# Expert list sorted within each half of the tokens in a two-layer decoder kernel

## What is computed

```python
def hier_moe(h, w_group, b_group, w_expert, b_expert, w_gate, w_up, w_down):
    ...
    g_idx = jnp.argmax(g_logits, axis=-1)                  # 1 of 4 groups
    e_prob = jax.nn.softmax(e_logits[rows, g_idx], axis=-1)
    top_p, top_i = lax.top_k(e_prob, TOP_K)                # 2 of its 8 experts
    top_p = top_p / jnp.sum(top_p, axis=-1, keepdims=True)
    weights = g_w[:, None] * top_p
    expert_id = g_idx[:, None] * EXPERTS_PER_GROUP + top_i
    ...
        xb = t[tok]                                        # the tokens of expert e
        y = (jax.nn.silu(xb @ w_gate[e]) * (xb @ w_up[e])) @ w_down[e]
        return y * wt[:, None].astype(y.dtype)
    ...
    out = jax.ops.segment_sum(ys.reshape(P, D), tok_buf, num_segments=N)
```

## Time and profile before

| | |
|---|---|
| Median of 3 runs | 1249.63 us (1246.39 to 1251.85) |
| The profiled execution | 1250.87 us, span 1249.1 us from its first to its last instruction |
| Mean granted clock of PE | 0.970 of full speed |
| PE busy | 1176.5 us, 94% |
| DVE busy | 695.7 us, 56% |
| ACT busy | 326.3 us, 26% |
| Read from HBM | 240.19 MB |

### The profile page before, as it was taken

How to read it: one execution, slowest core, us unless ns; L and a number is a source line. 1 busy time by engine, 2 the same in 40 slices (tenths; PEclk the granted TensorE clock), 3 DMA queues, 4 the chain that set the end, 5 groups by cost and what they waited for, 6 DMA issues and landing times.

```text
span 1249.1 us, 17564 instructions
## 1 busy us (share of the span) xinstructions
PE 1176.5 (94%) x5132; PEld 657.6 (53%) x5132; DVE 695.7 (56%) x1627; ACT 326.3 (26%) x731; POOL 46.3 (4%) x89
## 2 busy tenths in 40 slices
PE   6999999999789999999979999999996999999997
PEld 3854555456584444444448545555565934444443
DVE  3344664557675555555542365644676745555555
ACT  4225231023412222222142153211143122222221
POOL 7000000000005000000000000000000000000000
PEclk9999998999889999999989999989997999999999
DMA  9030013420305999999740300244004069999992
GB/s 298 25 121 15 1 45 89 184 88 1 132 37 172 387 423 421 423 421 423 296 146 4 132 1 1 68 135 202 1 1 169 1 273 422 422 421 422 421 422 120
DMA packets 52965, 243.14 MB, mean 195 GB/s; under 512 B 8480, under 2 KB 19008, under 8 KB 27552
## 3 DMA queue, kind: packets, MB, share of 16 engines
q1 hardware_dynamic: 49760, 240.40, 48.5%
q0 software_dynamic: 2560, 1.89, 0.8%
q10 hardware_dynamic: 576, 0.02, 0.0%
HBM read 240.19 MB, written 2.10 MB: 194 GB/s over the span
## 4 chain that ended last, share of the span: by engine, by line
PE 86%; DVE 7%; issue 2%; DVEq 2%; ACT 1%; DMA 1%; ACTq 0%; POOLq 0%
PE ps L2560 18%; PE ps L2146 10%; PE ps L2582 9%; PE ps L2372 8%; PE ps L2138 6%; PE ps L2531 5%; PE ps L2532 5%; PE ps L2116 4%; PE ps L2167 4%; PE ps L2517 2%; PE ps L2239 2%; PE ps L2420 2%; PE ps L2208 2%; PE ps L2516 2%; PE ps L2216 1%
## 5 line engine op out<-in xcount | busy, mean ns | idle before, releaser
L2560 PE MATMUL ps<-wgu,xw 128*64 128x512 f32 x1024 | 225.5, 593 | 1.2 <-issue 0.6
L1978 DVE TENSOR_TENSOR X<-ps,X 128x512 f32<-128x512 f32 x256 | 156.6, 683 | 12.5 <-issue 10.0
L2146 PE MATMUL ps<-hT,ring 128*128 128x512 f32 x352 | 157.6, 603 | 0.0
L2560 PEld LDWEIGHTS ps<-wgu,xw 128*64 128x64 f32 x1024 | 74.6, 137 | 145.9 <-issue 145.7
L2582 PE MATMUL ps<-wdn,hhT 128*64 128x512 f32 x512 | 120.1, 612 | 3.3 <-ACTq L1211 3.3
L2372 PE MATMUL ps<-ring,yT 128*128 128x512 f32 x256 | 119.4, 616 | 0.4 <-DVE X L1376 0.4
L2531 PE MATMUL ps<-yhi,Wt 128*128 128x512 f32 x256 | 106.5, 416 | 3.7 <-DVEq L1262 3.7
L2146 PEld LDWEIGHTS ps<-hT,ring 128*128 128x128 f32 x352 | 67.2, 195 | 77.6 <-issue 77.6
L2532 PE MATMUL ps<-ylo,Wt 128*128 128x512 f32 x256 | 100.9, 394 | 0.0
L1985 DVE TENSOR_TENSOR hh<-ps,silu 128x256 f32<-128x256 f32 x32 | 13.6, 425 | 126.9 <-ACTq L1205 126.9
L1996 DVE SCALAR_TENSOR_TENSOR ylo<-ps,ws,yhi 128x512 fp32r<-128x512 f32 x64 | 48.1, 751 | 63.9 <-ACTq L1221 63.9
(11 more groups left out here) (367 smaller groups left out, 1496.7 us busy)
## 6 DMA issues: line engine op xcount, KB each, us to landing
wgu<-in_w_gate SPq DMA_DIRECT2D x64, 1024.0 KB, 12.2
wgu<-in_w_up SPq DMA_DIRECT2D x64, 1024.0 KB, 14.4
wdn<-in_w_down SPq DMA_DIRECT2D x64, 1024.0 KB, 14.2
ring<-in_w_in SPq DMA_DIRECT2D x8, 1024.0 KB, 6.6
ring<-in_w_mix_out SPq DMA_DIRECT2D x12, 512.0 KB, 6.0
w_kv<-in_xa_w_kv SPq DMA_DIRECT2D x4, 1024.0 KB, 9.4
ring<-in_w_in SPq DMA_DIRECT2D x2, 2048.0 KB, 15.5
ring<-in_w_in SPq DMA_DIRECT2D x2, 1536.0 KB, 15.7
```

Source lines behind the costliest of these rows:

```text
L1978: tt(xh, bank, xh, ALU.add).then_inc(mfreed((what, n)), 1)
L2146: last = mm(bank, w[:, c, c0:c0 + P], hT[:, c, :], start=c == 0, stop=c == KD - 1)
L2560: last = mm(bank[r], xw[:, c, r], wgu[2 * parity + j][:, :, c, :], start=c == 0, stop=c == KD - 1)
```

## The change

The list is no longer sorted over all tokens. It is sorted within each half of the tokens: first all assignments of tiles 0 and 1, by expert, then those of tiles 2 and 3. So each half of the list has only its own two tiles as sources, and the gather makes 2 tiles x 8 groups x 2 parts = 32 products for each half. An expert's tokens then lie in two spans. `list_spans` writes for each expert the start of the first, the start of the second, and the count of the first (at most 64); ACT copies 64 columns from the first start, and then, over what lies behind the first span, 64 columns from the second start to the place given by the count (`from_first`, `from_second`). Beside this, DVE's order is another (the last two tiles' one-hots, `placed`, `overflow_tiles`, which computes two more columns), PE runs `slots()` behind step 0, `diag` and `ranked` lie elsewhere, and SP loads pair 1's weights at once. The diff, cut to its core:

```diff
-        xw = at("xw", [P, KD, P], F32, late + 4096)
...
+        xw = at("xw", [P, KD, 2, 2 * SLOTS], F32, late + 4096)
...
-        G = at("G", [P, 2, SEQ], F32R, late)
+        G = at("G", [P, 3, SEQ], F32R, late)
...
-                load_gate_up(l, 1, 1)
-                load_down(l, 1, 1, (0,))
-                multiplied(l, 0, ("wslot",))
-                load_down(l, 1, 1, (1,))
+                load_pair(l, 1, 1)
...
+                def from_first(j, e):
+                    s0 = act.value_load(spans[0:1, bass.ds(e, 1)], min_val=0, max_val=2 * SEQ)
+                    copy(xw[:, :, j, 0:SLOTS], xgT[:, :, bass.ds(s0, SLOTS)])
+
+                def from_second(j, e):
+                    s1 = act.value_load(spans[0:1, bass.ds(e + NE, 1)], min_val=0, max_val=2 * SEQ)
+                    n0 = act.value_load(spans[0:1, bass.ds(e + 2 * NE, 1)], min_val=0, max_val=SLOTS)
+                    copy(xw[:, :, j, bass.ds(n0, SLOTS)], xgT[:, :, bass.ds(s1, SLOTS)])
+
+                def windows_second(p):
+                    act.drain()
+                    for j in range(2):
+                        from_second(j, 2 * p + j)
+                    act.drain()
+                    act.nop().then_inc(S["xw_ready"], 1)
...
+                        wait_apart(act, S["G_used"], done(l, "G_used", 2))
+                        for j in range(2):
+                            from_first(j, j)
...
-                        windows(p + 1)
+                        for j in range(2):
+                            from_first(j, 2 * p + 2 + j)
...
                     act.nop().then_inc(S["hhT_ready"], 1)
+                    if ahead:
+                        windows_second(p + 1)
                     if isinstance(p, int) and p == 0:
+                        for k in range(2):
+                            bank = mfull(act, l, 0, ("places", k))
+                            copy(places[:, k], bank).then_inc(mfreed(("places", k)), 1)
+                            act.drain()
+                            act.nop().then_inc(S["places_ready"], 1)
...
-                copy(xw[:, :, SLOTS:2 * SLOTS], xgT[:, :, bass.ds(second, SLOTS)])
...
+                windows_second(0)
                 step_(0, 0, True)
...
+                nc.vector.tensor_tensor_scan(rt[:, 4, 1:n_lists], counted[:, 0:n_lists - 1],
+                                             rt[:, 2, NT:NT + n_lists - 1], 0.0, ALU.add, ALU.add)
                 dve.drain()
-                tt(r32(5), ranked_from, row(4).unsqueeze(1).to_broadcast([P, NT, NE]), ALU.add)
+                lists = rt[:, 4, 0:n_lists].rearrange("p (g e) -> p g e", g=HALVES)
+                tt(rt[:, 5].rearrange(by_half, g=HALVES, e=NE), ranked_from,
+                   lists.unsqueeze(2).to_broadcast([P, HALVES, NT // HALVES, NE]), ALU.add)
...
-                def one_hot(half, t):
-
-                    g = NT * half + t
-                    place = (dest, dest_2)[half]
-                    if g >= 2:
-                        dve.wait_ge(S["G_used"], done(l, "G_used", g - 1))
-                    ts(Gx[:], iota[:], place[:, 0, t:t + 1], None, ALU.is_equal)
-                    dve.drain()
-                    stt(G[:, g % 2], iota[:], place[:, 1, t:t + 1], Gx[:], ALU.is_equal, ALU.add)
+                def one_hot(t):
+
+                    place = (dest, dest_2)[t // (NT // HALVES)]
+                    hot = G[:, t % 3]
+                    if t >= 3:
+                        dve.wait_ge(S["G_used"], done(l, "G_used", t - 2))
+                    ts(hot, iota[:], place[:, 0, t:t + 1], None, ALU.is_equal)
+                    dve.drain()
+                    stt(hot, iota[:], place[:, 1, t:t + 1], hot.bitcast(F32), ALU.is_equal, ALU.add)
                     signal("G_ready")
...
+                def list_spans():
+
+                    dve.wait_ge(S["rank_kept"], done(l, "rank_kept", 1))
+                    ts(rt[:, 4, n_lists:n_lists + NE], first_count, float(SLOTS), None, ALU.min)
+                    tt(counts, first_count, rt[:, 1, NE:2 * NE], ALU.add)
+                    tt(rank[:, 2:4], rank[:, 2:4], first_count.unsqueeze(1).to_broadcast([P, 2, NE]), ALU.add)
+                    dve.drain()
+                    nc.vector.tensor_copy(spans, rt[:, 4, 0:3 * NE])
+                    signal("spans_ready")
...
+                    ts(expert, expert, float(NE - 1), None, ALU.min)
+                    for dst, of in ((first, first_from), (second, second_from), (split, split_from)):
+                        tt(passed, begun[:], of.unsqueeze(1).to_broadcast([P, OVF, NE]), ALU.mult)
+                        dve.drain()
+                        nc.vector.tensor_reduce(dst.unsqueeze(2), passed, AX_X, ALU.add)
...
                     if back:
                         bring_back(p, "comb", range(8))
                     else:
+                        placed()
+                        overflow_tiles()
                         slot_weights()
                         spread(parity)
                     for h in range(2):
...
-                one_hot(0, 0)
+                one_hot(0)
                 low_part(0)
-                one_hot(0, 1)
+                one_hot(1)
                 low_part(1)
                 ts(dest_2[:], dest[:], -float(SEQ), None, ALU.add)
-                nc.vector.tensor_copy(starts[:], row(4))
-                signal("starts_ready")
+                list_spans()
+                one_hot(2)
                 low_part(2)
-                one_hot(0, 2)
+                nc.vector.memset(xgT[:, :, 2 * SEQ:SORTED], 0.0)
+                sorted_gain(0)
                 low_part(3)
-                one_hot(0, 3)
+                one_hot(3)
+                sorted_gain(1)
+                tiles_past()
+                padded_places()
                 token_weights()
-                one_hot(1, 0)
-                sorted_gain(0)
-                one_hot(1, 1)
-                tiles_past()
-                one_hot(1, 2)
-                padded_places()
-                one_hot(1, 3)
-                nc.vector.memset(xgT[:, :, 2 * SEQ:SORTED], 0.0)
-                placed()
-                sorted_gain(1)
-                overflow_tiles()
                 step_(0, 0, False)
...
                 pe.wait_ge(S["rank_kept"], done(l, "rank_kept", 1))
-                for half in range(HALVES):
-                    for t in range(NT):
-                        if half == 0:
-                            wait_apart(pe, S["xhi_ready"], done(l, "xhi_ready", t + 1))
-                            if t > 0:
-                                wait_apart(pe, S["xlo_ready"], done(l, "xlo_ready", t + 1))
-                        pe.wait_ge(S["G_ready"], done(l, "G_ready", NT * half + t + 1))
-                        hot = G[:, t % 2]
-                        if t == 0:
-                            for c in range(KD):
-                                mm(mbank_of(l, 0, ("sorted", half, c)), xhi[:, t, c::KD], hot,
-                                   start=True, stop=False)
-                            if half == 0:
-                                wait_apart(pe, S["xlo_ready"], done(l, "xlo_ready", 1))
+                for t in range(NT):
+                    half, inner = t // per, t % per
+                    wait_apart(pe, S["xhi_ready"], done(l, "xhi_ready", t + 1))
+                    pe.wait_ge(S["G_ready"], done(l, "G_ready", t + 1))
+                    hot = G[:, t % 3]
+                    if inner == 0:
                         for c in range(KD):
-                            bank = ps[:, head.job["sorted", half, c][0], :]
-                            if t > 0:
-                                mm(bank, xhi[:, t, c::KD], hot, start=False, stop=False)
-                            last = mm(bank, xlo[:, t, c::KD], hot, start=False, stop=t == NT - 1)
-                            if t == NT - 1:
-                                last.then_inc(mfilled(("sorted", half, c)), 1)
-                        if t < NT - 1:
-                            last.then_inc(S["G_used"], 1)
-                        else:
-                            pe.drain()
-                            pe.nop().then_inc(S["G_used"], 1)
+                            mm(mbank_of(l, 0, ("sorted", half, c)), xhi[:, t, c::KD], hot, start=True, stop=False)
+                    wait_apart(pe, S["xlo_ready"], done(l, "xlo_ready", t + 1))
+                    for c in range(KD):
+                        bank = ps[:, head.job["sorted", half, c][0], :]
+                        if inner > 0:
+                            mm(bank, xhi[:, t, c::KD], hot, start=False, stop=False)
+                        last = mm(bank, xlo[:, t, c::KD], hot, start=False, stop=inner == per - 1)
+                        if inner == per - 1:
+                            last.then_inc(mfilled(("sorted", half, c)), 1)
+                    if inner < per - 1:
...
+                step_(0, 0, False)
                 slots()
-                step_(0, 0, False)
```

113 lines of the change are left out of this document (56 added, 57 removed).

## The result

The changed kernel takes 1234.54 us (median of 5 runs, 1226.14 to 1235.26) against 1249.63 (1246.39 to 1252.03) for the kernel before on the same chip: ratio 0.9863, interval 0.9838 to 0.9888. That is faster by 1.4%, inside the range that I gave and 2.8 us above the time that I named. Run a second time, beside the first three experiments, it gave 1233.85 (6 runs) and a ratio of 0.9856 [0.9829, 0.9883].

What follows compares the result with a forecast made beforehand. PE was taken to bound the kernel (86% of the last chain), the gather being its own. Twice -8.3 a layer plus 1.3 from transfers makes 17.9 us off 1250.87: 1233.0, named 1231.7 as median; range 1225 to 1239, chance 0.85.

Steps and rivals of the forecast that it cites:

- The sum per layer: Start of pair 1 in each layer: -14.7 + 4.7 + 1.7 = -8.3 us.
- Products removed and the gather's end: Gather on PE: 64 of 128 products go, 15.7 us; with stalls and drains the gather ends 14.7 us earlier per layer.
- The wait for ACT: Ahead of pair 0's gate/up: PE idles 4.9 us for ACT's copies and register loads, 4.7 more than before.
- The clock in that gap: PE's new empty gap ends at the low clock, costing 1.7 us on pair 0's gate/up, 8.7 instead of 7.05.
- The gap behind gate/up stays and pays its 1.69 as before: Pair 0's down products stay at the slow clock, 5.27 us against 3.58 in the loop.
- Step 0 on DVE: Overflow part grows to 9 us; `ylo` of pair 0 ready after 16.6, wanted after 19.1: covered, 2.4 to spare.
- signs of being wrong: Wrong if PE waits on `xw_ready` in the loop, or on `ylo_ready` in step 1.
- DVE's tail in step 0 is longer than its cover: Rival: overflow part 12 us, pair 1 waits 0.6, clock falls again, 2.3 a layer: 1236.3; chance 0.12 (shared with longer stalls).
- The loop: ACT's two more copies a pair cost nothing, with 0.7 us to spare before PE needs `xw_ready`; step stays 14.58.
- The transfers: Pair 2's load gains 3.7 us of lead, recovering the late last pairs' loss at the loop's end: 1.3 us in all.
- The 0.6 for `wgu`: Pair 15 of layer 0 waits 0.6 us for `wgu`, read as the transfers being late at the loop's end.
- DVE holds the gather's end: Rival: gather ends where it did, PE's saving turns into waits, 11.5 us slower, 1261; chance 0.02.

Runs made afterwards that it cites:

- first three experiments: placed_early, act_regs and pe_fill, edits of the changed kernel timed beside its second run; medians 1231.44, 1227.35 and 1231.08 us.
- act_regs: Changed kernel with pair 0's four second-window register loads moved on ACT to behind the wait for the spans; 1227.35 us, ratio to before 0.9802.
- pe_fill: Changed kernel plus 16 unread products on PE between the last gather product and the wait for xw_ready; 1231.08 us, ratio to before 0.985.
- slots_first: Changed kernel with slots() ahead of step 0 on PE again and placed() ahead of it on DVE; 1250.81 us, ratio to before 0.9999.
- combo: Changed kernel with placed_early, act_regs and no_drain joined, and xgT's tail memset moved behind one_hot(3) on DVE; 1223.15 us, ratio to before 0.9775.
- placed_early: Changed kernel with placed() moved on DVE to ahead of step 0; 1231.44 us, ratio to before 0.9852.
- fill_both: Changed kernel with pe_fill's 16 products and nine more unread products behind pair 0's gate/up; 1231.52 us, ratio to before 0.9834.
- no_drain: Changed kernel without PE's drain and signal ahead of the last pair's step, SP waiting for the same event instead; 1232.12 us, ratio to before 0.9857.
- more_copies: Changed kernel with ACT copying the second windows of pairs 1 to 15 twice, behind a drain; 1253.37 us, ratio to before 1.0015.
- late_load: Changed kernel with SP issuing pair 2's loads only when PE has done slots(); 1245.62 us, ratio to before 0.9961.

## Why the prediction was right, and which of its terms were not

The sum per layer was -8.3 us; to the start of pair 2 it was measured at -8.8 (67.62 to 58.83) and -8.7 (67.51 to 58.78). With the late steps that is 18.0 us, where the sum had 17.9; the medians are 15.1 and 17.0 apart, and what lies outside the two stretches varies by 7.8 us between two executions of the changed kernel (726.1 and 733.9). Point by point:

*Products removed and the gather's end*: -14.7 predicted, -14.5 measured (33.72 to 19.25). The stalls are where I put them: tile 2's eight products took 3.36 instead of 1.96, and PE waited 0.40 for the last one-hot.

*The wait for ACT*: 4.9 predicted, 4.40 measured, gate/up 23.65 us after the first gather product where I had 23.9. act_regs shows that the register loads are part of it.

*The clock in that gap*: gate/up 8.7 predicted, 8.76 to 8.79 measured, and once 9.25; pe_fill shows that the idle gap is the cause.

*"The gap behind gate/up stays and pays its 1.69 as before"*: **this step failed.** Down took 3.65 and not 5.27. The runs show one fall for the two gaps: where the first was filled, the second paid (pe_fill, 5.35 twice; before, 5.27 and 5.24), where the first paid, the second did so in two of twelve, and where both were filled none did. (slots_first, with its other order, has a long gate/up and a long down in layer 0, 9.54 and 4.98; in layer 1 `slots()` alone is long, 5.8.) In act_regs neither paid, with gaps of 2.60 and 2.96 us (the two small products within it counted), and combo's gap of the same 2.60 fell in one layer of two. So the length of a gap in these rows doesn't decide it alone. The Trainium skill's page "TensorE: Matmul & The Clock Gate", section on the HAM clock gate, has the monitor's window running freely, so that where the clock changes differs from run to run. With that, combo's two layers agree; why a fall in the first gap mostly spares the second stays open.

*Step 0 on DVE, "covered, 2.4 to spare"*: **this step failed too**, by the same 1.7 us the other way. The overflow part took 9.4 (9 predicted). The 19.1 us of cover held the slow down products; with down at 3.65, PE asks for `ylo` 17.2 us behind the end of gate/up (375.89 to 393.13) and DVE has it at 17.4, not 16.6. So one of my signs of being wrong came, a wait on `ylo_ready` in step 1: 0.36 us in each layer. And the cover was reckoned to `ylo` alone. The spread, `hh` of pair 1 and the additions to `X` stand behind it on DVE, and PE wants them in the middle of step 1. Step 1 took 16.27; placed_early shows the place, pe_fill and fill_both the size. The rival "DVE's tail in step 0 is longer than its cover" came in part, by another route than the 12 us that it asks for. Each miss is some 3.3 us over both layers. That they cancel has a mechanism, which the prediction didn't have: DVE takes 19.1 us from `hh` of pair 0 to `hh` of pair 1, and a shorter down only leaves PE more to wait (no_drain, layer 1). That this row is just as long as PE's path with the slow down (step 1 is 14.65 in pe_fill, 14.58 is a step of the loop) is luck; a longer one would have come on top of the sum.

*The loop*: nothing predicted, with 0.7 to spare; the steps are 14.56 to 14.59. The margin is about 0.3: the copies end 3.5 us behind `hhT` (3.7 predicted), but more_copies shows PE starting only 0.5 behind the end of the last copy, which the sum had at next to nothing. ACT's idle time ahead of `yhi` went from 3.04 us to 0.41.

*The transfers*: 1.3 predicted, 0.5 measured. The term is mis-sized because I took all that the step to the last pair has above 14.58 (15.30 and 15.14 in my reading; 15.35 and 15.31 between the starts in the timeline) for transfers. The drain is most of it (no_drain). The 0.6 for `wgu` is that same idle time: it stands in layer 1 as well, and in the changed kernel, where no transfer is late. Only the two steps of 14.64 and 14.92 and 0.1 of the last in layer 0 were theirs. late_load shows that the lead itself is what I took it for.

*The rival "DVE holds the gather's end"* did not come, but something close to it is near: slots_first shows that what DVE does behind the gather (6.6 us of places and weights, then `placed()`) eats the whole gain as soon as PE asks for it ahead of pair 0. With the 64 products gone, the gain still hangs on `slots()` standing behind step 0.

## What to carry to other kernels

Where products are taken away from the bounding engine, walk to the next thing that each of the other engines owes, past the first wait: ask not only when the result it waits for is ready but what stands in the same queue behind it and who wants that. Two costs that run side by side (a slow clock on one engine, a long queue on another) can hide each other; undo them one at a time and together before you put a price on either. And where PE and the transfers are as close as here (14.58 and 14.91 us a step), some of what is saved ahead of a loop can come back in its last steps (0.5 to 1.1 us in four of these profiles, always in layer 0): compute the pace of the transfers (bytes of a step by the rate of the windows) before counting on the next microsecond.

## What the runs showed of the hardware that was not expected

- Of two gaps of PE with 8.8 us of work between them, the granted clock fell mostly in one only: in the first of them (4.4 us, empty) in 12 of 12 cases, in the second (1.1 and 1.4 us with two small products between) in 2 of 12, but in 4 of 4 where the first gap was absent or filled and the second was not. With the first filled too, nine unread products in the second kept it up in 4 of 4. A first gap of 2.6 us fell in 1 of 4.
- Two register loads on ACT ahead of a copy idle it by 0.57 to 0.73 us, and with a drain ahead of them by 1.5; moving four loads to an idle stretch took 1.8 us off a wait.
- From the end of ACT's last copy to PE's start on its result passed 0.52 us, a drain and a signal (more_copies).
- A drain and a signal on PE between two steps cost 0.55 us of idle PE and about 0.7 in all.
- Where the weight loads set the pace, the 16 DMA engines moved 422 GB/s at a share of 1.01 (late_load and combo, windows of three and five steps; 435 in one window of 4.5 us). With POOL's small transfers beside them they moved 349 in late_load and 337 before, at a share of 1.03. The Trainium skill's page "Perfetto Trace Analysis", section on engine utilization, gives about 120% of a core's 358 GB/s share as the practical ceiling where a single core is active; 422 is 118% of it, so the trace agrees.
